# Rounded, wider position products, two spare products and an earlier first pick at the experts' entry of a decoder step

## The reference

```python
def moe_swiglu(h, w_router, w_gate, w_up, w_down):
    t = h.reshape(-1, shape[-1])                       # 256 or 32 rows of 1024
    logits = (t @ w_router).astype(jnp.float32)        # 8 experts
    top_logits, top_idx = lax.top_k(logits, TOP_K_EXPERTS)
    gates = jax.nn.softmax(top_logits, axis=-1)
    combine = jnp.sum(jax.nn.one_hot(top_idx, N_EXPERTS) * gates[..., None], axis=1)
    for e in range(N_EXPERTS):
        out = out + combine[:, e:e + 1] * swiglu(t, w_gate[e], w_up[e], w_down[e])
```

## Time and profile before

| | us |
|---|---|
| median of 3 timed runs | 1501.34 |
| lowest, highest | 1501.07, 1503.48 |
| profiled execution, its own time | 1506.59 |
| its span, first to last instruction | 1504.9 |
| TensorE busy (8176 products) | 1492.0 |
| VectorE busy | 1194.8 |
| ScalarE busy | 974.9 |
| GpSimd busy | 157.1 |
| HBM read and written | 456 MB |

### The profile page before, as it was taken

The page is one execution under the profiler, slowest core; times in us unless marked ns, Lnnn a source line. Parts: engine busy times, 40 slices in busy tenths (PEclk is TensorE's granted clock), DMA queues, the critical chain, the costliest instruction groups (busy, mean ns, idle before and its releaser), DMA issues.

```text
span 1504.9 us, 21505 instructions
## 1 busy us (share of the span) xinstructions
PE 1492.0 (99%) x8176; PEld 1271.4 (84%) x8176; DVE 1194.8 (79%) x1083; ACT 974.9 (65%) x930; POOL 157.1 (10%) x160
## 2 busy tenths in 40 slices
PE   9999999999999999999999999999999999999998
PEld 7887789999988988888888888888888888888887
DVE  4689667665555768888888888889888888888987
ACT  4443554443455477777777777777778777777775
POOL 3554000000000048001001001001000000000100
PEclk9999999999999989999999999999999999999999
DMA  7651994345564379999999999999999999999990
GB/s 219 234 227 57 357 337 153 114 153 211 182 200 168 116 227 373 392 394 383 394 393 382 395 377 372 394 378 359 393 391 358 397 393 370 379 393 367 374 357 32
DMA packets 198854, 456.91 MB, mean 304 GB/s; under 512 B 12020, under 2 KB 15134, under 8 KB 198794
## 3 DMA queue, kind: packets, MB, share of 16 engines
q1 hardware_dynamic: 190802, 439.34, 78.9%
q0 software_dynamic: 4336, 13.15, 3.1%
q10 hardware_dynamic: 3656, 3.60, 0.8%
HBM read 444.04 MB, written 12.03 MB: 303 GB/s over the span
## 4 chain that ended last, share of the span: by engine, by line
PE 93%; DVE 4%; ACT 1%; issue 1%; DMA 0%; ACTq 0%; DVEq 0%
PE bank L2013 22%; PE bank L2529 13%; PE bank L2531 13%; PE bank L2530 13%; PE bank L2543 7%; PE bank L2545 7%; PE bank L2544 7%; PE bank L2553 2%; PE bank L2000 1%; PE bank L2206 1%; DVE rt L1570 1%; PE bank L2101 1%; PE bank L2497 1%; PE bank L2218 1%; PE bank L2299 0%
## 5 line engine op out<-in xcount | busy, mean ns | idle before, releaser
L1798 DVE TENSOR_TENSOR wql<-ring,wqh 128x2048 fp32r<-128x2048 f32 x335 | 766.6, 2291 | 110.3 <-ACT wqh L985 109.3
L985 ACT ACTIVATE wqh<-ring 128x2048 fp32r<-128x2048 f32 x334 | 641.2, 1920 | 233.0 <-PE bank L2531 150.6
L2529 PE MATMUL bank<-wqh,xgh 128*128 128x512 f32 x892 | 353.6, 396 | 0.4 <-DVE wql L1798 0.4
L2530 PE MATMUL bank<-wql,xgh 128*128 128x512 f32 x896 | 349.8, 390 | 0.0
L2531 PE MATMUL bank<-wqh,xgl 128*128 128x512 f32 x892 | 348.0, 390 | 0.0
L2531 PEld LDWEIGHTS bank<-wqh,xgl 128*128 128x128 f32 x892 | 167.4, 188 | 35.9
L2530 PEld LDWEIGHTS bank<-wql,xgh 128*128 128x128 f32 x896 | 168.9, 188 | 32.9
L2529 PEld LDWEIGHTS bank<-wqh,xgh 128*128 128x128 f32 x892 | 167.6, 188 | 34.4 <-DVE wql L1798 1.2
L985 ACT ACTIVATE wd<-ring 128x1024 fp32r<-128x1024 f32 x90 | 95.2, 1059 | 133.2 <-PE bank L2013 133.0
L2543 PE MATMUL bank<-wqh,heTh 128*128 128x512 f32 x440 | 171.4, 389 | 0.0
L2545 PE MATMUL bank<-wqh,heTl 128*128 128x512 f32 x440 | 171.2, 389 | 0.0
(11 more groups left out here) (452 smaller groups left out, 1986.4 us busy)
## 6 DMA issues: line engine op xcount, KB each, us to landing
ring<-in_moe_w_gate SPq DMA_DIRECT2D x56, 2048.0 KB, 11.3
ring<-in_moe_w_up SPq DMA_DIRECT2D x56, 2048.0 KB, 12.1
ring<-in_moe_w_down SPq DMA_DIRECT2D x56, 2048.0 KB, 11.7
ring<-in_attn_w_in SPq DMA_DIRECT2D x7, 2048.0 KB, 12.7
ring<-in_ffn_w_gate SPq DMA_DIRECT2D x5, 2048.0 KB, 15.6
ring<-in_ffn_w_up SPq DMA_DIRECT2D x5, 2048.0 KB, 10.6
ring<-in_cache_k SPq DMA_DIRECT2D x16, 512.0 KB, 7.0
ring<-in_cache_v SPq DMA_DIRECT2D x16, 512.0 KB, 6.1
```

The lines of the kernel that those rows point to most:

```text
L985: return nc.scalar.activation(dst, src, ACT.Copy)
L1798: return v.tensor_tensor(dst, src, head.bitcast(F32), ALU.subtract)
L2529: mm(bank, xgh[:, k, :], w_h[:, part], start=(k == 0), stop=False)
L2530: mm(bank, xgh[:, k, :], w_l[:, part], start=False, stop=False)
```

## The change

- `sel` becomes a tile of 96 columns per row tile (`SELW`) in the rounded type. Its first 8 columns hold what `sel` held; GpSimd sets the others to zero once. `ones` and `upper` get the rounded type too. The position products read all 96 columns and write 96 columns per result, now as one pass each; DVE reads the first 8 of each.
- Ahead of TensorE's wait for `sel`, two spare products of 512 columns run into the bank `pos`, whose content the position products then overwrite.
- On DVE `rows_tail(0, 0)` and `rows_tail(1, 0)` move behind `picks(0)`.

```diff
+SELW = 96
...
-    ones = sb("ones", [P, P])
+    ones_r = sb("ones", [P, P], F32R)
+    ones = ones_r[:].bitcast(F32)
...
-    upper = sb("upper", [P, P])
+    upper_r = sb("upper", [P, P], F32R)
+    upper = upper_r[:].bitcast(F32)
...
-    sel = sb("sel", [P, 3, E], stack=moe)
+    sel_wide = sb("sel", [P, 3, SELW], F32R, stack=moe)
+    sel_r = sel_wide[:, :, 0:E]
+    sel = sel_r.bitcast(F32)
...
-        for t, v in ((lg, MARK), (l8, MARK), (sel, 0.0), (slot_of, -FAR)):
+        nc.gpsimd.memset(sel_wide[:].bitcast(F32), 0.0)
+        for t, v in ((lg, MARK), (l8, MARK), (slot_of, -FAR)):
...
-        v.tensor_scalar(sel[:, 0:2, :], wk[:, 0:2, 0:E], MARKED, None, ALU.is_lt)
-        v.tensor_scalar(sel[0:NS, 2, :], wk[0:NS, 2, 0:E], MARKED, None, ALU.is_lt).then_inc(sel_ok, 1)
+        v.tensor_scalar(sel_r[:, 0:2, :], wk[:, 0:2, 0:E], MARKED, None, ALU.is_lt)
+        v.tensor_scalar(sel_r[0:NS, 2, :], wk[0:NS, 2, 0:E], MARKED, None, ALU.is_lt).then_inc(sel_ok, 1)
...
-
-        rows_tail(0, 0)
-        rows_tail(1, 0)
...
-        v.scalar_tensor_tensor(out=pos[:, 0:2, :], in0=B.ap("pos")[:, 0:2 * E].rearrange("p (m e) -> p m e", m=2),
+        v.scalar_tensor_tensor(out=pos[:, 0:2, :], in0=B.ap("pos")[:, 0:2 * SELW].rearrange("p (m e) -> p m e", m=2)[:, :, 0:E],
...
-        v.tensor_copy(cnt[:, 0:E], B.ap("pos")[:, 3 * E:4 * E]).then_inc(cnt_ok, 1)
+        v.tensor_copy(cnt[:, 0:E], B.ap("pos")[:, 3 * SELW:3 * SELW + E]).then_inc(cnt_ok, 1)
...
         picks(0).then_inc(pick_ok, 1)
+        rows_tail(0, 0)
+        rows_tail(1, 0)
         rows_tail(2, 0)
...
         B.room(pe, "pos")
+        spare(B.ap("pos"), ones_r[:], ones_r[:].unsqueeze(1).broadcast_to([P, 4, P]), 2)
         pe.wait_ge(sel_ok, 1)
...
-                left = upper[0:kr, 0:r] if k == m else ones[0:kr, 0:r]
-                last = mm(B.ap("pos")[0:r, E * m:E * m + E], left, sel[0:kr, k, :], start=(k == 0), stop=(k == parts[-1]))
+                left = upper_r[0:kr, 0:r] if k == m else ones_r[0:kr, 0:r]
+                last = mm(B.ap("pos")[0:r, SELW * m:SELW * m + SELW], left, sel_wide[0:kr, k, :], start=(k == 0), stop=(k == parts[-1]))
```

More of the change, by code:

```diff
@@ L836, in _ @@
         memsets((upper[:], 1.0))
-        select(upper[:], ALU.is_ge, 0.0, -1, [[1, P]], -1)
+        select(upper_r[:], ALU.is_ge, 0.0, -1, [[1, P]], -1)
         nc.gpsimd.iota(iota[:], [[1, P]], base=0, channel_multiplier=0, allow_small_or_imprecise_dtypes=True)
@@ L898, in two @@
             link(nc.gpsimd.tensor_tensor(dst, a_, b_, op))
-        slot0, weight, chosen = slot_of[:, :, 0:E], comb[:, :, 1:1 + E], sel[:].bitcast(F32)
+        slot0, weight, chosen = slot_of[:, :, 0:E], comb[:, :, 1:1 + E], sel[:]
         link(nc.gpsimd.tensor_scalar(flat[:], slot0, float(P), float((E - 1) * P), ALU.is_ge, ALU.mult))
@@ L1862, in _ @@
         dve.wait_ge(*B.full("pos"))
-        v.scalar_tensor_tensor(out=pos[:, 0:2, :], in0=B.ap("pos")[:, 0:2 * E].rearrange("p (m e) -> p m e", m=2),
+        v.scalar_tensor_tensor(out=pos[:, 0:2, :], in0=B.ap("pos")[:, 0:2 * SELW].rearrange("p (m e) -> p m e", m=2)[:, :, 0:E],
                                scalar=FAR, in1=sel[:, 0:2, :], op0=ALU.add, op1=ALU.mult)
-        v.scalar_tensor_tensor(out=pos[0:NS, 2, :], in0=B.ap("pos")[0:NS, 2 * E:3 * E], scalar=FAR, in1=sel[0:NS, 2, :],
+        v.scalar_tensor_tensor(out=pos[0:NS, 2, :], in0=B.ap("pos")[0:NS, 2 * SELW:2 * SELW + E], scalar=FAR, in1=sel[0:NS, 2, :],
                                op0=ALU.add, op1=ALU.mult).then_inc(b_dve, 1)
-        v.tensor_copy(cnt[:, 0:E], B.ap("pos")[:, 3 * E:4 * E]).then_inc(cnt_ok, 1)
+        v.tensor_copy(cnt[:, 0:E], B.ap("pos")[:, 3 * SELW:3 * SELW + E]).then_inc(cnt_ok, 1)
         dve.wait_ge(*B.freed("pos"))
```

## The result

The change made the kernel slower: 1527.43 us against 1501.2 us (medians of four runs each), a ratio of 1.0153 (95% interval 1.0126 to 1.0181). The forecast was 1495.3 us, with a range of 1494.0 to 1501.6. The changed kernel's profiled execution took 1524.23 us. Of all executions behind this document one is left out of every median, the profiled one of run e3, which took 3634.52 us with its products some 618 ns apart at a granted clock of 1.00, for a reason that no run shows.

A forecast was written before the change was run, and what follows sets the result against it. TensorE was taken as the bound, at half clock for 13.64 us at the experts' entry. About 5 us from the clock and 1 from positions and pick made 6.0: 1501.34 - 6.0 = 1495.3 us, range 1494.0 to 1501.6.

The forecast's parts named there:

- behind it the order of work is unchanged on every engine: After the start of the second half tile, every engine's work keeps its order; the forecast followed the change only to there.
- A lead won here is therefore kept to the end: Time won at the experts' entry lasts to the kernel's end, since nothing downstream waits for a time of its own.
- the anchor: Start of the second half tile on TensorE, at 550.57 us before; forecast at 544.55, 6.0 us earlier.
- The one on the slower side: Rival: the half-clock stretch moves into the experts' products; 1501.3 us (tie) or 1507 us; chance 0.04.
- Spares in the wait, 0 us: Two spare products, 0.46 us, fit TensorE's 0.51 us idle gap ahead of the position products; cost 0 us.
- Nine position products, 1.0 us, end at 534.6: Nine one-pass position products at 0.112 us replace 18 records taking 2.04 us, ending 0.9 us earlier.
- The rule that would have made them 42 ns apart: Skill's N/2.4 GHz plus about 2.5 ns spacing, at 96 columns; position products would end about 0.6 us sooner still.
- Pick done at 536.15: DVE starts positions at about 534.65, ahead of the low rows, and ends the pick 1.2 us earlier.
- DVE through at 540.85, first half tile 541.6, second 544.55: After the pick, DVE's chain ends about as before; first half tile starts 4.5 us earlier, second 6.0.
- The clock stays full through the entry: Filled pause and wider position products keep TensorE's full clock through the entry; about 5 of the 6.0 us gain.
- The timed median holds the low stretch, as the profile does: The 5.25 us between profile and median is profiling's cost, so the median gains the full 6.0 us; chance 0.50.
- The first rival: Timed runs had no half-clock stretch at the entry; gain only 0.2 us, 1501.1 us; chance 0.29.

The follow-up runs named there:

- e3: Kernel before with an unused tile of 32 bytes per partition behind `sel`; 1528.44 us, ratio 1.0168.
- e1: Kernel before with an unused tile of 1056 bytes per partition behind `sel`, no instruction changed; 1527.14 us, ratio 1.0168.
- e14: Kernel before with gaps of 32 bytes behind `sel` and 224 ahead of `xtok`, moving the stationary tiles against both moving ones; 1527.77 us, ratio 1.0171.
- e10: Changed kernel with row tiles of `sel` 92 columns apart, tiles behind it 1024 bytes later instead of 1056, measured once more; 1502.4 us, ratio 0.9997.
- e12: Changed kernel with 92-column row tiles and the two low-row subtractions ahead of the positions again; 1504.61 us, ratio 1.0013.
- e11: Changed kernel with 92-column row tiles, without the two spare products; 1501.27 us, ratio 0.9992.
- e2: Changed kernel with row tiles of `sel` 92 columns apart, so tiles behind it move 1024 bytes instead of 1056; 1501.49 us, ratio 0.9999.
- e15: Kernel before with gaps of 32 bytes ahead of `wqh` and 224 behind it, so only `wqh` moves modulo 256; 1515.63 us, ratio 1.0091.
- e6: Kernel before with 32 unused bytes ahead of `wql` only; 1518.4 us, ratio 1.0104.
- e7: Kernel before with 32 unused bytes ahead of `wqh`, moving all experts' operands together; 1503.56 us, ratio 1.0002.

## Why the prediction was wrong

**The step that failed** is the first of the part on the change: "behind it the order of work is unchanged on every engine", and with it, from the part on what bounds the kernel, "A lead won here is therefore kept to the end". The order is unchanged; the durations are not. The term that I put at nothing was the pace of the products behind the anchor: I had taken every one of them as before, at about 227 ns, and of the wider `sel` I had costed only the products that read it, not what it does to the places of the tiles behind it. Measured: +22.9 us behind the anchor, and e1 gives 22.8 us of it from the gap alone. Why these distances cost time is open. None of my rivals held it. The one on the slower side put its loss in the clock.

The Trainium skill, "TensorE: Matmul & The Clock Gate", section "Step-by-step: what each phase is for", says that the stationary and the moving operand are read through separate ports, so that loading the next weights takes no read bandwidth from the running product. No run here shows the ports. What the runs show is that the pace isn't free of how the two operands lie to each other: 32 bytes between the tiles cost 4 to 8 ns per product (e1, e14).

Point by point:

- *Spares in the wait, 0 us.* Right: the first position product starts at 533.41, before it was 533.42.
- *Nine position products, 1.0 us, end at 534.6.* Nearly: 0.11 us apart as taken, end at 534.78. The rule that would have made them 42 ns apart did not hold here.
- *Pick done at 536.15.* Late by 0.84, as DVE's timeline shows (answers to the earlier trace rows; the last row is the end of its chain):

```profile
534.93 0.17 DVE L1866 SCALAR_TENSOR_TENSOR pos<-bank,sel 128x16 f32<-128x16 f32 x1 [1.30 <-PE bank L2488]
...
535.68 0.60 DVE L1874 COPY slot_of<-slot_of 32x8 f32<-32x8 f32 x1
536.31 0.68 DVE L1881 TENSOR_SCALAR pick<-iota,slot_of 128x128 fp32r<-128x128 f32 x3
...
541.57 0.14 DVE L1898 TENSOR_SCALAR cnt_i<-r 1x1 int32<-1x1 f32 x1
```

  The positions begin 0.3 us later than I had them (534.93 against 534.65), and one small copy took 0.60 us, where the same copy took 0.20 before. I had no term for it. Why the copy took longer is open.
- *DVE through at 540.85, first half tile 541.6, second 544.55.* Measured 541.71, 542.36 and 545.22: 0.7 to 0.9 us late, from the pick on. The gain was 5.35 us where I had 6.0, and both are gains over a profile with the long stretch.
- *The clock stays full through the entry.* Right in this profile and in e10's. But my reason was only half of it: I argued from the columns of the products and the filled pause, and e12, which has both, fell to half level all the same, while e11 held the clock without the spares. I gave the order on DVE no part in the clock, and it has one.
- *The timed median holds the low stretch, as the profile does.* Wrong, and this would have failed the forecast even with the tiles in place. The first rival had it right, and e2 measured 1501.49 us where it gave 1501.1. Its gain of 0.2 us was too much: with the clock kept on both sides the new entry is 0.30 us slower (e10 against e15). Its old side was nearly right (anchor 11.50 us behind the first position product, where it had 11.33), its new side 0.7 us early. That the profiled execution lay 5.25 us above the median was the stretch itself and not the price of profiling: by the entries above the stretch costs 5.0 us (17.15 - 12.19) to 5.65 (17.15 - 11.50), and e10's profiled execution, without a stretch, took 1500.99 us, less than the median of its series. The argument that I set against it was that three runs without the stretch were unlikely. With 14 of 61 runs at that level it was about an even chance (0.77 x 0.77 x 0.77 = 0.46).

## What to carry to other kernels

When a tile changes its size, list the addresses of all tiles behind it before costing anything else, and compare the operands of the dominant products pair by pair; here distances of 32, 64 and 128 bytes cost 0.4 to 1.9%, and a gap padded to 256 or 1024 left the pace as it was. To judge such a change, compare the time of the stretch that the change doesn't touch. When one profiled execution differs from the median by just the price of something seen in it, look into the timed runs before assuming that the median holds it too. An entry that the clock depends on is judged by how often the low level comes, not by one profile, and by a profile of the old entry at the full clock.

## What the runs showed of the hardware

- The start-to-start time of rounded products of 128 x 128 by 512 columns, at the full clock, was 227 ns with moving and stationary tiles at the same place modulo 256 bytes, and medians of 226 to 237 ns otherwise. The patterns are the same in the two traces of one layout (the change and e1), and free of what DVE and ACT do. Over the whole kernel that was 0.4% (128 bytes) to 1.9% (64 bytes); behind the anchor it was 6.2 to 27.1 us of 954.3.
- A product's pace also changes when only tiles of its neighbours move (e6, e15).
- The length of the half-level stretches at the entry varied between executions and layouts of the same instructions: 13.64 us before, 6.8 us in e1's profile, 3.4 us in e7's, none in e15's.
